# Two-block transformer kernel on one Trainium2 core: the value products of the softmax branch with high and low parts in one stationary operand

## What is computed

```python
o = g[..., 0:1] * to_bshd(o_cmp) + g[..., 1:2] * to_bshd(o_slc) + g[..., 2:3] * to_bshd(o_win)
```

```python
s = jnp.einsum('bghqd,bgkd->bghqk', qb, kwb)
p_win = masked_softmax(s, mw)
o_win = jnp.einsum('bghqk,bgkd->bghqd', p_win, vwb.astype(jnp.float32))
```

## Time and profile before

| | |
|---|---|
| Three runs, median (lowest, highest) | 1585.1 us (1583.49, 1589.44) |
| The profiled execution | 1588.07 us |
| Its span | 1586.3 us |
| Busy: TensorE, VectorE, ScalarE, GpSimd | 1503.0, 837.7, 686.8, 203.5 us |
| Matmuls | 8601, each with a weight load |
| Mean granted clock of TensorE | 0.98 |

### The profile page before, as it was taken

How to read it: one execution, slowest core, us unless ns; L and a number is a source line. 1 busy time by engine, 2 the same in 40 slices (tenths; PEclk the granted TensorE clock), 3 DMA queues, 4 the chain that set the end, 5 groups by cost and what they waited for, 6 DMA issues and landing times.

```text
span 1586.3 us, 22143 instructions
## 1 busy us (share of the span) xinstructions
PE 1503.0 (95%) x8601; PEld 1262.0 (80%) x8601; DVE 837.7 (53%) x1444; ACT 686.8 (43%) x1305; POOL 203.5 (13%) x308
## 2 busy tenths in 40 slices
PE   4999998999989999999999999988999999999997
PEld 2788866678988888888888886768988888888986
DVE  5767645577454444432275445775644444432364
ACT  4555545377443222221353235786542232222453
POOL 0000000244310000000130013553300000000111
PEclk9999999899999999999999999999999999999998
DMA  9533330002223333333403321003033333333321
GB/s 373 211 100 100 120 146 9 1 2 85 76 59 101 93 95 103 93 94 100 139 1 114 99 84 76 1 1 107 1 88 98 93 96 102 93 106 100 114 80 54
DMA packets 40387, 143.06 MB, mean 90 GB/s; under 512 B 4448, under 2 KB 6512, under 8 KB 39792
## 3 DMA queue, kind: packets, MB, share of 16 engines
q1 hardware_dynamic: 38240, 129.55, 26.1%
q0 software_dynamic: 1488, 11.52, 1.9%
q10 hardware_dynamic: 576, 0.85, 0.2%
HBM read 139.81 MB, written 2.10 MB: 89 GB/s over the span
## 4 chain that ended last, share of the span: by engine, by line
PE 82%; DVE 7%; ACT 5%; issue 3%; DMA 1%; POOL 1%; SPq 0%; DVEq 0%; ACTq 0%; POOLq 0%
PE B L276 24%; PE B L278 23%; PE B L277 23%; PE B L1635 2%; PE B L1853 2%; PE B L1517 2%; ACT T L548 1%; PE B L1719 1%; PE B L1614 1%; DVE WADA L1057 1%; POOL T L469 1%; DVE X L1022 1%; DMA X<-in_x 1%; DVE WL L1011 1%; DVE KEPT_L L1009 1%
## 5 line engine op out<-in xcount | busy, mean ns | idle before, releaser
L276 PE MATMUL B<-UH,WH 128*128 128x512 f32 (+1 forms) x1120 | 421.7, 377 | 15.5 <-DVE UL L1066 5.7
L278 PE MATMUL B<-UH,WL 128*128 128x512 f32 (+1 forms) x1120 | 417.8, 373 | 0.0
L277 PE MATMUL B<-UL,WH 128*128 128x512 f32 (+1 forms) x1120 | 417.6, 373 | 0.0
L276 PEld LDWEIGHTS B<-UH,WH 128*128 128x128 f32 x1120 | 213.3, 190 | 56.6 <-DVE UL L1029 8.0
L548 ACT ACTIVATE WH<-RAW 128x1024 fp32r<-128x1024 f32 x178 | 186.6, 1051 | 136.9 <-DMA RAW<-in_stream 116.7
L278 PEld LDWEIGHTS B<-UH,WL 128*128 128x128 f32 x1120 | 213.0, 190 | 36.5
L277 PEld LDWEIGHTS B<-UL,WH 128*128 128x128 f32 x1120 | 213.3, 190 | 36.1
L1011 DVE TENSOR_TENSOR WL<-RAW,WH 128x1024 fp32r<-128x1024 f32 x98 | 121.9, 1246 | 165.2 <-ACT WH L548 165.0
L548 ACT ACTIVATE T<-B 128x256 f32<-128x256 f32 (+3 forms) x207 | 96.0, 466 | 128.8 <-PE B L278 62.6
L1311 DVE TENSOR_TENSOR WL<-RAW,WH 128x1024 fp32r<-128x1024 f32 x80 | 98.1, 1226 | 76.7 <-ACT WH L548 73.9
L548 ACT ACTIVATE T<-T 128x512 f32<-128x512 f32 (+3 forms) x131 | 68.6, 525 | 139.2 <-DVE T L1315 119.2
(11 more groups left out here) (334 smaller groups left out, 2962.6 us busy)
## 6 DMA issues: line engine op xcount, KB each, us to landing
RAW<-in_stream SPq DMA_DIRECT2D x202, 512.0 KB, 3.6
WADA<-in_w_ada SPq DMA_DIRECT2D x4, 2048.0 KB, 18.8
RAW<-in_stream SPq DMA_DIRECT2D x16, 384.0 KB, 3.4
WADA<-in_w_ada SPq DMA_DIRECT2D x4, 1024.0 KB, 18.4
W<-in_w POOLq DMA_DIRECT2D x2, 2048.0 KB, 11.1
X<-in_x SPq DMA_DIRECT2D x2, 1024.0 KB, 11.1
DECAY<-in_decay POOLq DMA_DIRECT2D x1, 2048.0 KB, 8.1
X<-in_x POOLq DMA_DIRECT2D x2, 1024.0 KB, 8.1
```

What stands on the lines that cost most here:

```text
L276: nc.tensor.matmul(out, lh, rh, start=start, stop=False, **kw)
L277: nc.tensor.matmul(out, lh, rl, start=False, stop=False, **kw)
L278: return nc.tensor.matmul(out, ll, rh, start=False, stop=stop, **kw)
```

## The change

The values get one tile VN, in which the 64 columns of the high part and the 64 of the low part stand side by side, for each block of keys and each (kind, group). A block's value product is two matmuls: low weights x high values (64 stationary columns, rows 0 to 63 of the bank), and high weights x both parts (128 stationary columns, all 128 rows of the bank). So the bank's lower half collects high x low alone. BD gets 128 columns, of which 64 to 127 are zero, and opens all 128 rows. When a head is done, ScalarE copies rows 0 to 63 as before, and VectorE then adds rows 64 to 127 (new event `at_sum`); what waited for `at_x` on TensorE and in the multiplication now waits for `at_sum`.

```diff
-        VNH, VNL = hb("VNH", 88, [P, 4, 256], F32R), hb("VNL", 92, [P, 4, 256], F32R)
+        VN = hb("VN", 88, [P, 4, 4, 2, HD], F32R)
...
-        BD = hb("BD", 57, [P, 2, 4, HD])
-        KCF = hb("KCF", 59, [P, 4, 32])
+        BD = hb("BD", 57, [P, 2, 4, P])
+        KCF = hb("KCF", 61, [P, 4, 32])
...
-            o = slice(kind * P + g * HD, kind * P + (g + 1) * HD)
...
-                    "v": lambda b: (VNH[:, b, o], VNL[:, b, o])}
+                    "both": lambda b: VN[:, b, 2 * kind + g, :, :]}
...
-                            E["v_hi"].mark(f(VNH[:, t, :], B[4 + t][:, 0:256], ACT.Copy))
+                            E["v_hi"].mark(f(VN[:, t, :, 0, :], B[4 + t][:, 0:256].rearrange("p (c e) -> p c e", c=4), ACT.Copy))
...
-                            E["v_lo"].mark(tt(VNL[:, t, :], B[4 + t][:, 0:256], VNH[:, t, :], ALU.subtract))
+                            E["v_lo"].mark(tt(VN[:, t, :, 1, :], B[4 + t][:, 0:256].rearrange("p (c e) -> p c e", c=4), VN[:, t, :, 0, :], ALU.subtract))
...
-                        E["cmp_bd"].mark(v.tensor_copy(BD[rows, g, j, :], B[6][rows, P + HD * g:P + HD * (g + 1)]))
+                        E["cmp_bd"].mark(v.tensor_copy(BD[rows, g, j, 0:HD], B[6][rows, P + HD * g:P + HD * (g + 1)]))
...
-                        chain.done(v.tensor_copy(KP[:, :, :], BD[:, :, :, :].rearrange("p g j e -> p (g j e)").rearrange("p (j c) -> p j c", j=4)))
+                        chain.done(v.tensor_copy(KP[:, :, :], BD[:, 0, :, :]))
...
             def nsa_ahead(m):
+                if m >= 12 and (m - 12) % 8 == 0:
+                    j = (m - 12) // 8
+                    for s in range(2):
+                        rows = pair_rows(j)
+                        wait(dve, at_x, 2 * j + s + 1)
+                        at_sum.mark(tt(T[10 + s][rows, :], B[s][HD:P, :], T[10 + s][rows, :], ALU.add))
                 if m in (20, 36):
                     for s in range(2):
                         p = m // 36 + 2 * s
-                        wait(dve, at_x, 4 * (m // 36) + 3 + s)
+                        wait(dve, at_sum, 4 * (m // 36) + 3 + s)
...
                             for b in range(i + 1):
+                                if units is NSA_UNITS:
+                                    at = slice(b * P, (b + 1) * P)
+                                    mat(B[s][0:HD, i * P:(i + 1) * P], x["both"](b)[:, 0, :], AL2[:, u % 4, at],
+                                        start=False, stop=False, skip_group_check=True)
+                                    ins = mat(B[s][:, i * P:(i + 1) * P], x["both"](b), AH2[:, u % 4, at],
+                                              start=False, stop=b == i, skip_group_check=True)
+                                    continue
...
-                    wait(pe, at_x, 2 * (m // 8 - 1) + s + 1)
-                    mat(B[s][0:HD, :], BD[:, s, m // 8, :], PTC[:, s, :], start=True, stop=False, skip_group_check=True)
+                    wait(pe, at_sum, 2 * (m // 8 - 1) + s + 1)
+                    mat(B[s][:, :], BD[:, s, m // 8, :], PTC[:, s, :], start=True, stop=False, skip_group_check=True)
...
-                        bank_free=lambda m: wait(pe, *((NSA["exp"], 62), (NSA["exp"], 62), (at_x, 7), (at_x, 8), (NSA["lo"], 64), (NSA["exp"], 64))[m]),
+                        bank_free=lambda m: wait(pe, *((NSA["exp"], 62), (NSA["exp"], 62), (at_sum, 7), (at_sum, 8), (NSA["lo"], 64), (NSA["exp"], 64))[m]),
```

More of the change, by code:

```diff
@@ L290, in build @@
             "pt_hi pt_lo pp ep pl_s".split())}
-        pl_y, at_x, at_m, at_hi, at_lo = (Event(n) for n in "pl_y at_x at_m at_hi at_lo".split())
+        pl_y, at_x, at_sum, at_m, at_hi, at_lo = (Event(n) for n in "pl_y at_x at_sum at_m at_hi at_lo".split())
         f_g, f_s, f_u, f_h, f_hh, f_hl = (sem(n) for n in "f_g f_s f_u f_h f_hh f_hl".split())
```

## The result

The changed kernel takes 1589.33 us in the median of 12 runs (1585.7 to 1595.31), the kernel before 1586.12 us in 12 runs on the same chip (1583.49 to 1589.44). The ratio is 1.0024, with a 95% interval of 1.0014 to 1.0034: 3.8 us more, where 2.7 were forecast. The profiled execution has a span of 1591.5 us and took 1593.43 us.

A forecast was written before the change was run, and what follows sets the result against it. TensorE was taken to bound the kernel, busy 80.80 of the softmax branch's 82 us. Terms -1.4 + 0.2 + 2.2 + 0.5 + 1.2 = +2.7 us gave 1587.8 us from 1585.1, range 1582.0 to 1592.0.

The forecast's parts named there:

- value products: TensorE's 160 value blocks: 170 ns each instead of 180, 1.6 us gained, 1.4 counted because the last 20 wait anyway.
- compressed product: TensorE's product with widened BD: second load covered, first costs 50 ns more at four odd halves, 0.2 us lost.
- sums before the compressed product: TensorE waits for VectorE's sum, not ScalarE's copy, at three head pairs: 0.62 + 0.74 + 0.62 + 0.18 = 2.2 us.
- VectorE's lateness behind pair 1: Two steps after pair 1, VectorE's low parts come late and hold TensorE's transposes: 0.5 us more.
- stage end: Two sums ahead of VectorE's last multiplications push the chain TensorE waits for: 1.2 us, uncovered.
- clock: TensorE's granted clock at the stage's end: waits under a microsecond had not lowered it, so no term was charged.
- the memset's cover: BD's memset doubles from 0.48 to 0.96 us; VectorE's 1.31 us idle before 265.73 hides it, costing nothing.
- The first: Rival: matmul count sets the time, the wide load hides; 50 ns more gained per block, 8.0 us, 1579.8; chance 0.09.
- The second: Rival: sums don't reach TensorE, costing near 0.35 us each; the 2.2 and 0.5 fall to about 0.7, 1585.8; chance 0.12.
- the fourth: Rival: alternating 64 and 128 columns costs extra on TensorE; at 80 ns a switch 25.6 us, 1613; chance 0.04.
- The fifth: Rival: the wide load takes 120 ns, blocks stay at 180, the 1.4 us gain is missing: 1589.2; chance 0.10.
- The third: Rival: VectorE's lateness does not heal across three head pairs; 1.5 to 3.9 us instead of 0.5, 1589 to 1591; chance 0.08.

The follow-up runs named there:

- e1: The changed kernel without VectorE's eight additions, their waits back on ScalarE's copies: 1583.91 us against 1586.0 for the kernel before, ratio 0.9986.
- e7: The kernel before with only the compressed product widened to 128 stationary columns, 64 of them zero: 1583.67 us against 1586.59, ratio 0.9982.
- e6: The changed kernel with six unused 512-column matmuls filling TensorE's wait at the stage's end: 1587.64 us, ratio 1.0008 to the kernel before.
- e2: The kernel before with each block's third product (high weights x low values) left out, two 64-column matmuls remaining: 1579.3 us, ratio 0.9954.
- e4: e1 with a third 64-column matmul (low weights x low values) added to each block: 1590.39 us, ratio 1.0027 to the kernel before.
- e3: The kernel before plus eight VectorE maxima of the sums' shape, with the changed kernel's waits: 1589.1 us, ratio 1.002.

## Why the prediction was right, and where its steps were not

The total was forecast as +2.7 us and came out as +3.8 by the ratio, +3.2 by B. The account of the stage, from the views above:

| step | forecast | measured | from |
|---|---|---|---|
| value products | -1.4 | -0.8 | A of e1 less A of e7 |
| compressed product | +0.2 | -1.7 | e7: 1.45 and 0.29 |
| sums before the compressed product | +2.2 | +2.2 | below |
| VectorE's lateness behind pair 1 | +0.5 | +0.7 | below |
| stage end | +1.2 | +1.4 | 1.96 against 0.59 us idle |
| clock | none | +1.5 | 3.97 against 2.47 us; e6 |
| sum | +2.7 | +3.3 | stage: +3.2 |

The first two rows rest on differences between runs and take it that the compressed product gains in the changed kernel what it gains in e7 (its first step does: 1.03 and 1.04 us). The third and the fourth come from the changed kernel beside e1, which differ by the sums alone: from the second compressed product to the third it takes 20.09 us (e1 19.42), from head pair to head pair 21.36 (20.57) and 22.23 (20.84), and from the last to the projection 16.55 (16.50). That is 0.67, 0.79, 1.39 and 0.05 us. The 1.39 can be parted at the row of 353.98, where TensorE waits for the low parts behind pair 1: up to there it is 4.01 us from pair 1's compressed product (e1 3.28), and from there to pair 2's 18.22 (17.56). So 0.73 us are the lateness and 0.66 the sum of pair 2, and the three sums come to 0.67 + 0.79 + 0.66 + 0.05 = 2.17.

**Right.** The block of 60 + 110 = 170 ns, and with it the sentence that the widened load eats five sixths of a removed matmul: e2 (120 ns) and e4 (230 ns) confirm the two prices one by one. The sum's 0.69 us and its three waits were right to 0.1 us in 2.2, and VectorE's lateness turned up in the one place that was named, with 0.7 us for 0.5. So were the memset's cover (VectorE's idle time of the earlier trace rows fell from 1.31 to 0.78 us, and no wait moved out), and the wait at the end of the stage, 1.37 for 1.2. From the second compressed product to the matmul behind that wait it is 2.0 us more (86.72 for 84.71), at the low end of the 2 to 3 that were named.

**Wrong: the compressed product.** The prediction said "its second load is covered" and charged 0.2 us for the first. It priced the widened operand by its own load alone and took it for granted that the narrow one let the next load through. The operand ahead of a load matters too: the value product's load stood idle for 0.81 us behind the narrow product. The rows of before held the sign: from compressed product to compressed product in the timeline of before it is 1.33 us, where the prediction's two matmuls "in about 1 us" and three of 60 ns make 1.2.

**Wrong: the clock.** "Waits under a microsecond have not lowered the granted clock" was true and did not bear on the case, as the prediction itself made of that wait one of about 2 us. The kernel before shows that the clock can fall behind such waits: at the stage's opening TensorE is idle for 1.87 us before 300.00 and, eight matmuls later, for 0.66 before 301.43, and the granted clock is 0.75 in the window of 300 to 303 us and 0.68 in the next 3. The prediction took no price from these windows:

```profile
300.00:303.00 3.00, 2.34 (x15) 1.44 (x16) 0.86 (x5) 1.99 (x8) 2.30 (x4) 0.75 0.00 0
303.00:306.00 3.00, 3.00 (x22) 2.17 (x22) 2.47 (x8) 2.27 (x7) 0.85 (x2) 0.68 0.00 0
```

There the clock fell behind two idle stretches close together, and e3, with a single one of 1.89 us, kept the full clock. So these rows were a warning, not a rule.

**Mis-sized: the value products.** The 10 ns a block are there, 1.6 us over 160. The five waits of about 0.16 us for low parts and 0.04 more at the place of the earlier trace rows take back 0.8. The prediction excepted only the last 20 blocks; VectorE's low parts came late once in every head pair, not in the last alone.

**The rivals.** The first (the matmul count sets the time, 1579.8) falls: e4 has the old count and is slower. So does the estimate of 81 ns for each pair of load and matmul, from the Trainium skill's "TensorE: Matmul & The Clock Gate", section "Back-to-back issue gap": the rows show 60 and 110. The second (the sums don't reach TensorE) falls by the three rows, the fourth (a price for switching widths) by the 170 ns. The fifth has the nearest time, 1589.2, with a wrong cause: a block takes 170 ns, not 180. The Trainium skill's rule of columns divided by 1.2 (the same page, section "LDWEIGHTS (loading the stationary operand)") gives no gain for 192 columns against 192; the rows show 10 ns. The third found a place of a sort: lateness between head pairs does heal, but the faster TensorE meets VectorE's low parts once in every head pair.

So a forecast 1.1 us short of the ratio's 3.8 had 1.9 us wrong in one term, and 1.5 and 0.6 the other way in two others. That the total came as near as it did is in part luck: a gain that the prediction did not see paid for a loss that it did not see either. The total alone would not have told.

## What to carry to other kernels

Where the moving side is as short as here (128 columns), count a fused operand by its load columns, not by matmuls saved: 64 + 128 columns cost 170 ns where three loads of 64 cost 180, so fusing them needs a follow-up that costs nothing on the path, and here eight additions of 0.69 us cost more than it gave. With 256 moving columns the matmuls of the projection, on 128 stationary ones, start 0.12 us apart, 10 ns more than with 128: there the moving side fills nearly all of the time that the wide load takes. Look at what a narrow f32 operand does to the load behind it; filling its spare columns with zeros paid 0.2 us a product here, and a kernel that does only this beats both. Where an edit lengthens a wait of TensorE, look for what the clock did behind waits of that length in the trace, and take a fall as a rival with a price (here 1.5 us).

## What the runs showed of the hardware that was not expected

- A two-matmul f32 product of 512 columns, with a value product behind it, takes 1.33 us with 64 stationary columns, 1.04 with 96 and 1.04 with 128. The next operand's load starts 1.01 us after the product does in the first case, 0.44 in the last.
- At the stage's end, 1.96 to 1.98 us without a matmul was followed by the level of 1.2 GHz for about 3 us and cost 1.5 us, in three profiles of three; 1.89 and 1.90 us were not, in two of two. With six matmuls of no use in that wait the clock stayed at 1.00.
- VectorE's addition of 64 partitions by 512 elements, one side in PSUM, takes 689 ns, as on 128 partitions (692): half the partitions are no cheaper.
- A 128-column operand in front of 128 moving columns takes 110 ns in fp32r and 60 ns in bf16; a 64-column one in fp32r 60 ns.
